# A two-block transformer layer on one core: memory and x loaded in both orientations, x's norm factor moved behind the products

## The chip, the core and the metric

The kernel runs on one core of a Trainium2 chip. The metric is the device time of one execution in microseconds (us). The engines in what follows are TensorE (PE in the profile; its weight loads are PEld), VectorE (DVE), ScalarE (ACT), GpSimd (POOL) and SyncE (SP), whose queue issues all loads and stores here.

## The reference, cut to what matters

Two transformer blocks on 256 tokens of width 1024, all in float32. Only the start of the first block is touched by the change:

```python
def rms_norm(x, g):
    xf = x * lax.rsqrt(jnp.mean(x * x, axis=-1, keepdims=True) + RMS_EPS)
    return xf * g

h = rms_norm(x, mix_norm_g)                    # x: 256 x 1024
proj = h @ w_in                                # 1024 x 4800
u_pool, q_down, kv_down, k_rope_in, xq, gate_logits = jnp.split(proj, ...)
y_pool = pool_mixer(u_pool, pool_w, pool_scale)
y_mla  = mla_branch(q_down, kv_down, k_rope_in, cos, sin, ...)
kv     = rms_norm(mem, mem_norm_g) @ w_mem_kv  # mem: 256 x 1024
y_mem  = memory_cross_attention(xq, kv)        # 4 heads of 128
gates  = sigmoid(gate_logits + gate_b)
x = x + (gates[0] * (y_pool @ w_br_pool) + gates[1] * (y_mla @ w_br_mla)
         + gates[2] * (y_mem @ w_br_mem)) @ w_out
x = x + hierarchical_moe(rms_norm(x, ffn_norm_g), ...)   # 32 experts, 2 per token
return second_block(x, ...)                    # attention and a gated FFN
```

## The kernel before, in words

**Arithmetic.** A float32 product is made of three passes over rounded halves: an operand a is split into a high part (rounded) and a low part (a minus the high part), and high x high, low x high and high x low are summed in PSUM. For weights, ACT makes the high half (`wh`, line 1309) and DVE the low half (`wl`, line 1720), a *piece* of up to 1024 columns at a time. There are four places for pieces (`PIECES`), so the split of piece n waits until TensorE has used piece n-4. In the program text `split_to(n)` splits all pieces up to n, and `stream(key)` walks over the pieces of one matrix and stays three pieces ahead (`AHEAD`).

**Orders.** Each engine has its own program and runs it strictly in order; semaphores named after the points they mark (`up`, `at`) tie them together. SP issues the weight loads in one list (`fetch(u)`), a unit being up to 1 MB. There are five raw places (`DENSE`), and from the sixth unit on `fetch` waits until DVE has made the last `wl` of the unit that held the place.

**The start.** `mem` comes as four column blocks of 256 KB into `H`, between the first four weight units. TensorE transposes each block (`turn_memory`, line 757), ACT and DVE make the halves `mT` from PSUM, scaled by the norm's gain G (lines 1358 and 1731), and `memory_keys` (line 777) multiplies the first half of `w_mem_kv` with them: four pieces, called 0 to 3 here. The token norm factor of `mem` is not in `mT`. It is applied where results leave PSUM: as a row for the keys (`spread` puts the factors on a diagonal on DVE, TensorE multiplies ones with it, and `spread_row` copies the row out), and as a scale for the values. Pieces 4 to 7 are the value half of `w_mem_kv`, pieces 8 to 11 are the columns `xq` of `w_in`, and after them come `qd`, `kvd` and the rest.

**x before.** x is loaded whole to `X`. ACT sums its squares (line 1318), POOL makes the factor (lines 2343 and 2346), DVE multiplies x by it into `H` (line 1824), TensorE transposes `H` in two groups of four tiles (line 645), and ACT and DVE make the halves `hT` from PSUM.

**The rotation's angles.** POOL makes the factors of mem and x first, in this order, and then computes the angles of the rotary embedding in some 24 small steps (lines 2361 to 2382). ACT takes their sine (line 1428). In ACT's program the sine stands after `whole(stream(("mkv", 1)))` and before `whole(stream("xq"))`, so the casts of the last xq piece and of the pieces after it stand behind the sine.

**Later stages.** The latents, the cross attention, the pooling and the gates of the first block, the experts (whose 100 MB are loaded while TensorE works), and the second block, which are not touched except for the places where x's factor now enters.

Of the kernel before, what the change touches and what calls it, by code (L numbers as in the profile page):

```python
# [26 lines left out]
MEM_AT = ((4, 0), (5, 0), (6, 0), (7, 0), (2, 0), (3, 0), (4, 1), (5, 1))  # L27
X_AT = ((4, 0), (5, 0), (6, 0), (7, 0), (4, 1), (5, 1), (6, 1), (7, 1))
# [170 lines left out]
def weights(a):  # L199
# [13 lines left out]
    wt.split(("mkv", 0), first[:, 0:2], first[:, 2:4], *(r[:, z:z + 2] for r in rest for z in (0, 2)))  # L213
# [65 lines left out]
def build(nc, wt, x, mem, positions, gate_b, w_gate_e, w_up_e, w_down_e, grow, w_route, b_route, rel_ext, cst, dense,  # L279
          out, force_general=False):  # L280
    with ExitStack() as ctx:
        program(nc, ctx, x, mem, positions, gate_b, grow, w_route, b_route, rel_ext, cst, out, wt, dense, w_gate_e, w_up_e,
                w_down_e, force_general)


def program(nc, ctx, x, mem, positions, gate_b, grow, w_route, b_route, rel_ext, cst, out, wt, dense,
# [27 lines left out]
    memory = H.rearrange("p i n -> p (i n)").rearrange("p (c m) -> p c m", c=4)  # L314
    memory_rows = memory.rearrange("p c (i n) -> p i c n", i=2)
# [44 lines left out]
    fr = [big[:, a:a + 64].rearrange("p (i c) -> p i c", i=2) for a in (8000, 8064, 8128)]  # L360
# [71 lines left out]
    def released(u):  # L432

        if wt.units[u][2]:
# [4 lines left out]
    s_load = {n: sem("s_" + n) for n in ("ident", "mem0", "mem1", "mem2", "mem3", "cst", "x", "pos", "gate0", "gate1",  # L439
                                         "gfin", "wr", "br", "pm", "pf", "bias", "out")}  # L440
# [12 lines left out]
    rr = rms("pre")[1][:, 2:4]  # L453
    krow = rt[:, 64:320]
# [28 lines left out]
    def sync(e, real):  # L483
# [34 lines left out]
        xs, ov = (v.rearrange("a (i p) n -> p (a i) n", p=P) for v in (x, out))  # L518
# [8 lines left out]
        load("cst", C[:, C_TRI:C_END], cst[:, C_TRI:C_END])  # L527
        load("pos", posi[:, :], positions)
        load("br", brow, b_route.to_broadcast([P, 36]))
# [35 lines left out]
        for u in range(DENSE, wt.dense_end):  # L565
# [42 lines left out]
    def tensor(e, real):  # L608
# [142 lines left out]
        def turn_memory(c):  # L751

            e.wait_ge(*have(f"mem{c}"))
            for k in (2 * c, 2 * c + 1):
                enter(MEM_AT[k][0], "lo", "mem", k)
                for i in range(2):
                    t = e.transpose(rows_at(MEM_AT[k])[:, P * i:P * i + P],
                                    memory_rows[:, i, c, P * (k % 2):P * (k % 2) + P], ident)
            t.then_inc(*up("turn", "mem", 2 * c))

        def memory_keys(c):


            q = wt.run["mkv", 0][c]
            h, l = halves(q)
            e.wait_ge(*at("wh", q))
            for n, (w, y) in enumerate(((h, mT[0]), (h, mT[1]), (l, mT[0]))):
                if n == 2:
                    e.wait_ge(*at("wl", q))
                for kk in range(2):  # L770
                    k = 2 * c + kk
                    if n < 2:
                        e.wait_ge(*at(("hi", "lo")[n], "mem", k))
                    for j in range(4):
                        if n == k == j % 2 == 0:
                            enter(j // 2, "kept xk", j // 2)
                        t = e.matmul(bank[j // 2][:, 256 * (j % 2):256 * (j % 2) + 256], w[:, kk, P * j:P * j + P], y[:, k],  # L777
                                     start=(n == k == j % 2 == 0), stop=(n == 2 and k == 7), skip_group_check=True)
                if n == 0 and c < 3:
                    turn_memory(c + 1)  # L780
# [5 lines left out]
        e.wait_ge(*have("ident"))  # L786
        turn_memory(0)
        warm(WARM[1], 0)
        for c in range(4):
            memory_keys(c)  # L790
        vals = tokens(("mkv", 1), 1, mT, ("kept", "xv"))
        next(vals)
        e.wait_ge(*have("cst"))
        spread("mem row", 4)
        next(vals)
# [1694 lines left out]
```

## Time and profile before

| | |
|---|---|
| median of 3 runs | 784.41 us (784.09 to 784.75) |
| span of the profiled execution | 782.0 us |
| its matmuls (PE) | 735.6 us busy |
| its DVE, ACT, POOL | 419.5, 335.4, 30.0 us busy |
| bytes moved | 203.97 MB |
| mean granted TensorE clock, as a share of full speed | 0.987 |

The span goes from the first to the last instruction, and the median of the times is 2.4 us above it; no separate time of the profiled execution is listed. Busy time says how long an engine worked, and not whether anything waited for it; this is read from the chain of waits and from the timelines. Times in the trace count from the start of the span.

### The profile page before, as it was taken

What the parts mean: (1) busy time and instruction counts of PE and PEld (TensorE: products, weight loads), DVE (VectorE), ACT (ScalarE), POOL (GpSimd) and SP (SyncE); (2) the same over time, 40 slices, a digit from 0 to 9 for tenths busy, and PEclk for the clock granted to TensorE, in tenths of its full rate; (3) what the DMA queues carried; (4) which work ended last, traced back from release to release, by engine and by line L of the source; (5) the groups of instructions that cost most, each with busy time, mean ns of one, the idle gap of its engine ahead of it and who ended that gap; (6) DMA issues with size and microseconds to landing.
All of it is one profiled execution on the core that took longest, in us unless ns stands there. A gap on an engine that the chain in (4) does not pass through costs nothing.

```text
span 782.0 us, 12563 instructions
## 1 busy us (share of the span) xinstructions
PE 735.6 (94%) x5192; PEld 608.0 (78%) x5192; DVE 419.5 (54%) x747; ACT 335.4 (43%) x603; POOL 30.0 (4%) x64
## 2 busy tenths in 40 slices
PE   8999999999999999998766889999999999999997
PEld 8898888888788876665543559999878888888885
DVE  4758746667667421110100207766658776777675
ACT  6766565454444421110110117566556534344433
POOL 0700000000000000000000001100001000000001
PEclk9999999999999999999988999999999999999999
DMA  8762567347968899999999998963424464555201
GB/s 309 287 256 95 196 248 267 124 175 266 360 229 335 345 395 422 420 421 419 421 421 421 421 416 326 408 222 137 162 109 148 146 244 162 176 201 178 92 1 54
DMA packets 32010, 203.97 MB, mean 261 GB/s; under 512 B 3792, under 2 KB 4176, under 8 KB 9936
## 3 DMA queue, kind: packets, MB, share of 16 engines
q1 hardware_dynamic: 31952, 203.15, 66.9%
q8 instruction: 42, 0.69, 0.4%
q14 instruction: 16, 0.13, 0.1%
HBM read 202.09 MB, written 1.05 MB: 260 GB/s over the span
## 4 chain that ended last, share of the span: by engine, by line
PE 86%; DMA 8%; ACT 3%; DVE 2%; issue 1%; SPq 1%; DVEq 0%; POOLq 0%; POOL 0%; ACTq 0%
PE ps L658 45%; PE ps L727 10%; DMA ext<-in_w_up_e 7%; PE ps L1022 6%; PE ps L730 5%; PE ps L999 3%; PE ps L1057 2%; PE ps L1047 2%; PE ps L777 2%; PE ps L1149 1%; PE ps L1163 1%; PE ps L1177 1%; PE ps L621 1%; ACT wh L1309 1%; ACT big L1560 1%
## 5 line engine op out<-in xcount | busy, mean ns | idle before, releaser
L1720 DVE TENSOR_TENSOR wl<-raw,wh 128x1024 fp32r<-128x1024 f32 (+3 forms) x180 | 213.2, 1200 | 129.6 <-ACT wh L1309 128.4
L1309 ACT CAST wh<-raw 128x1024 fp32r<-128x1024 f32 (+3 forms) x180 | 182.0, 1029 | 63.2 <-PE ps L658 44.0
L658 PE MATMUL ps<-wh,fra 128*128 128x512 f32 (+3 forms) x668 | 189.4, 369 | 0.4 <-DVE gb L1934 0.4
L658 PEld LDWEIGHTS ps<-wh,fra 128*128 128x128 f32 x668 | 118.7, 189 | 19.2 <-issue 1.0
L658 PE MATMUL ps<-wl,fra 128*128 128x512 f32 (+3 forms) x334 | 121.5, 364 | 0.0
L727 PE MATMUL ps<-fra,wh 128*128 128x512 f32 x352 | 110.7, 396 | 0.7 <-DVE fra L1731 0.7
L730 PEld LDWEIGHTS ps<-fra,wl 128*128 128x128 f32 x352 | 66.1, 188 | 15.5
L658 PE MATMUL ps<-wh,frb 128*128 128x512 f32 x240 | 74.4, 391 | 0.0
L658 PE MATMUL ps<-fra,wh 128*128 128x256 f32 x400 | 73.8, 286 | 0.1
L658 PEld LDWEIGHTS ps<-wl,fra 128*128 128x128 f32 x334 | 62.9, 188 | 9.6
L730 PE MATMUL ps<-fra,wl 128*128 128x256 f32 x352 | 69.3, 278 | 0.0
L658 PEld LDWEIGHTS ps<-fra,wh 128*128 128x128 f32 x400 | 62.3, 192 | 1.0 <-issue 0.6
L2129 DVE TENSOR_TENSOR S<-S,ps 128x256 f32<-128x256 f32 x8 | 3.4, 422 | 107.5 <-ACT S L1570 107.5
L658 PE MATMUL ps<-fra,wl 128*128 128x256 f32 x200 | 56.6, 283 | 0.0
L727 PEld LDWEIGHTS ps<-fra,wh 128*128 128x128 f32 x352 | 54.3, 189 | 1.6 <-issue 0.9
L1570 ACT ACTIVATE S<-ps 128x256 f32<-128x256 f32 x8 | 3.1, 383 | 114.6 <-PE ps L1022 114.6
L658 PEld LDWEIGHTS ps<-wh,frb 128*128 128x128 f32 x240 | 44.1, 188 | 8.5
L658 PE MATMUL ps<-wl,frb 128*128 128x512 f32 x120 | 46.8, 390 | 0.0
L1022 PE MATMUL ps<-ext,big 128*32 128x256 f32 x384 | 34.9, 427 | 7.5 <-DMA ext<-in_w_up_e 7.5
L1022 PE MATMUL ps<-big 128*32 128x256 f32 x192 | 32.7, 429 | 9.1 <-DMA ext<-in_w_up_e 9.1
L658 PEld LDWEIGHTS ps<-fra,wl 128*128 128x128 f32 x200 | 38.3, 192 | 0.0
L1022 PE MATMUL ps<-raw,big 128*32 128x256 f32 x448 | 29.6, 381 | 5.7 <-issue 2.0
(269 smaller groups left out, 938.7 us busy)
## 6 DMA issues: line engine op xcount, KB each, us to landing
raw<-in_dense SPq DMA_DIRECT2D x79, 1024.0 KB, 5.0
raw<-in_w_gate_e SPq DMA_DIRECT2D x25, 1024.0 KB, 26.0
ext<-in_w_up_e SPq DMA_DIRECT2D x24, 1024.0 KB, 26.1
ext<-in_w_down_e SPq DMA_DIRECT2D x16, 1024.0 KB, 23.5
raw<-in_dense SPq DMA_DIRECT2D x16, 512.0 KB, 7.1
big<-in_w_up_e SPq DMA_DIRECT2D x8, 1024.0 KB, 20.7
raw<-in_w_down_e SPq DMA_DIRECT2D x4, 1024.0 KB, 19.6
gb<-in_w_down_e SPq DMA_DIRECT2D x4, 1024.0 KB, 20.8
```

What stands on the lines that cost most here:

```text
L621: e.matmul(bank[b][:, 0:P], src[:, 0:P], src[:, 0:P], start=True, stop=True)
L658: t = e.matmul(o, a, w, start=first and n == 0, stop=final and n == 2, skip_group_check=not check)
L727: e.matmul(bank[b][:, :], h[:, kk, cols[j]], hT_both[:, k], start=(k == 0), stop=(k == 7), skip_group_check=True)
L730: t = e.matmul(bank[b][:, 0:256], l[:, kk, cols[j]], hT[0][:, k], start=False, stop=(k == 7), skip_group_check=True)
L777: t = e.matmul(bank[j // 2][:, 256 * (j % 2):256 * (j % 2) + 256], w[:, kk, P * j:P * j + P], y[:, k], start=(n == k == j % 2 == 0), stop= ...
L999: t = e.matmul(bank[2 + a][:, P * (kk % 4):P * (kk % 4) + P], H[:, i, P * kk:P * kk + P], hot[:, P * i:P * i + P], start=(i == 0), stop=(i ...
L1022: t = e.matmul(bank[0][32 * j:32 * j + 32, 256 * half_:256 * half_ + 256], XE[:, kk, 32 * j:32 * j + 32], slot_view(wt.raws[key, 4 * g + j ...
L1047: t = e.matmul(bank[2 + c][32 * j:32 * j + 32, :], AT[z][:, P * k + 32 * j:P * k + 32 * j + 32], slot_view(wt.raws["ed", 4 * g + j])[:, k, ...
L1057: t = e.matmul(turned(k), YE[k // 4][:, P * (k % 4):P * (k % 4) + P], CM, start=False, stop=False, skip_group_check=True)
L1149: t = e.matmul(causal_parts(bank[4 + z])[i], qT[o:o + 64, k, P * i:P * i + P], kT[o:o + 64, k, 0:P * (i + 1)], start=True, stop=True)
L1309: e.copy(halves(q)[0], piece_view(q)).then_inc(*up("wh", q))
L1720: e.tensor_tensor(l, piece_view(q), h.bitcast(F), ALU.subtract).then_inc(*up("wl", q))
```

## The change

1. `mem` and `x` are each loaded twice: once turned by the host (`mem_t` in five parts of 1, 1, 2, 2 and 2 tiles of 256 columns; `x_t` in one load of 1 MB), and once in rows as before (`mem` whole, to `H`). This adds 2 MB of loads.
2. The halves `mT` and `hT` are made from the turned tiles in SBUF. TensorE's 32 transposes at the start and one group of warming matmuls (6 in the program) go.
3. `hT` no longer holds x's norm factor. The factor is applied at each place where a product of x leaves PSUM: as a row for the queries (a second `spread` and `spread_row`), as a scale for q's and kv's latents and for the pool input, in the gates' addition, and in the cosine and sine of the keys, which POOL multiplies once.
4. The first four weight tiles are units of 256 KB of their own, so that the keys have six pieces, 0 to 5. The values are then pieces 6 to 9, xq 10 to 13, and qd starts with 14.
5. SP's list at the start is new: x and `x_t` come later in it.

```diff
-    wt.split(("mkv", 0), first[:, 0:2], first[:, 2:4], *(r[:, z:z + 2] for r in rest for z in (0, 2)))
+    wt.split(("mkv", 0), *(first[:, z:z + 1] for z in range(4)), *(r[:, z:z + 2] for r in rest for z in (0, 2)))
...
-        load("mem0", memory[:, 0], mem[0])
+        fetch(0)
         load("ident", C[:, 0:C_TRI], cst[:, 0:C_TRI])
-        for c in range(4):
-            fetch(c)
-            if c < 3:
-                load(f"mem{c + 1}", memory[:, c + 1], mem[c + 1])
+        memory_tiles(0)
+        fetch(1)
+        memory_tiles(1)
+        fetch(2)
+        memory_tiles(2)
+        fetch(3)
         fetch(4)
+        memory_tiles(3)
+        fetch(5)
+        memory_tiles(4)
+        fetch(6)
+        load("mem", H[:, :, :], ms)
+        load("cst", C[:, C_TRI:C_END], cst[:, C_TRI:C_END])
+        load("cst", posi[:, :], positions)
+        load("cst", brow, b_route.to_broadcast([P, 36]))
+        fetch(7)
+        load("xT", xT.rearrange("p k n -> p (k n)"), x_t)
+        fetch(8)
         load("x", X[:, :, :], xs)
...
-        turn_tiles("x", H, X_AT, range(4), [at("scaled", "x", i) for i in range(2)])
         whole(vals)
-        turn_tiles("x", H, X_AT, range(4, 8), [at("scaled", "x", i) for i in range(2)])
-        whole(features("xq", 0, hT, ("kept", "xq"), row=("lo", "x")))
+        queries = features("xq", 0, hT, ("kept x", "q"), row=("lo", "x"))
+        next(queries)
+        next(queries)
+        spread("x row", 5)
+        whole(queries)
...
+        e.wait_ge(*have("xT"))
+        high_rows("x", hT[0], xT, range(4), G_MIX)
+        split_to(values[3])
+        high_rows("x", hT[0], xT, range(4, 8), G_MIX)
+        split_to(values[3] + 1)
         e.wait_ge(*have("x"))
         for i in range(2):
             e.wait_ge(*(own() if i else at("squared", "mem", 1)))
             square(rms("x")[0][:, i:i + 1], X[:, i, :], junk, "x", i)
...
-        for j in range(2):
-            keep(xqT[:, 2 * j:2 * j + 2, :], two(j), at("piece", last["xq"]), "xq", j)
...
+        queries = stream("xq")
+        next(queries)
+        next(queries)
+        e.wait_ge(*at("factor", "x", 0))
+        spread("x row", x_factor)
+        spread_row("x row", 5)
+        whole(queries)
+        for j in range(2):
+            e.wait_ge(*at("piece", last["xq"]))
+            e.tensor_tensor(xqT[:, 2 * j:2 * j + 2, :], bank[j][:, :].rearrange("p (j n) -> p j n", j=2),
+                            krow.unsqueeze(1).to_broadcast([P, 2, 256]), ALU.mult).then_inc(*up("kept x", "q", j))
...
-                e.tensor_tensor(g, bank[2 + i][:, :], gbt[n % 2], ALU.add).then_inc(*up("biased", n, i))
+                e.scalar_tensor_tensor(g, bank[2 + i][:, :], x_factor[:, i:i + 1], gbt[n % 2], ALU.mult, ALU.add).then_inc(
+                    *up("biased", n, i))
...
+        e.wait_ge(*at("sines"))
+        for i in range(2):
+            t = e.tensor_scalar(cs_k[:, :, i, :], cs[:, :, i, :], x_factor[:, i:i + 1], None, ALU.mult)
+        t.then_inc(*up("pool step", "sines of keys"))
```

How the order moves on ACT, from the xq casts' side: first before, then after the change. A cast is the high half of a piece, the activation with table load is the sine.

```order
L1309 CAST wh<-raw 128x1024 [waits p_piece,s_slot2]
L1358 ACTIVATE fra<-ps,C 128x256 [waits p_turn] x4
L1425 ACTIVATE big<-ps,st 128x512 [waits p_piece,p_factor]
L1425 ACTIVATE big<-ps,st 128x512 [waits p_piece]
L1428 ACT_TABLE_LOAD
L1428 ACTIVATE cs<-cs 128x128 [waits p_angles]
L1309 CAST wh<-raw 128x1024 [waits p_piece]
L1309 CAST wh<-raw 128x768 [waits p_piece,s_slot3]
```

```order
L1360 ACTIVATE fra<-big,C 128x256 [waits s_xT]
L1360 ACTIVATE fra<-big,C 128x256 x3
L1312 CAST wh<-raw 128x1024 [waits p_piece]
L1360 ACTIVATE fra<-big,C 128x256 x4
L1312 CAST wh<-raw 128x1024 [waits p_piece,s_slot3]
L1321 ACTIVATE junk,st<-X 128x1024 [waits p_squared,s_x]
L1321 ACTIVATE junk,st<-X 128x1024 [waits p_squared]
L1312 CAST wh<-raw 128x1024 [waits p_piece]
L1312 CAST wh<-raw 128x1024 [waits p_piece,s_slot4]
L1433 ACTIVATE big<-ps,st 128x512 [waits p_piece,p_factor]
L1433 ACTIVATE big<-ps,st 128x512 [waits p_piece]
L1436 ACT_TABLE_LOAD
```

x's squares now stand after the halves of the turned x and after the cast of piece 10, two casts and the values' scaling ahead of the sine; behind the sine the order is as it was.

On DVE, the low halves of the xq pieces: first before, then after the change. The two TENSOR_SCALAR on `rt` are the diagonal of x's factors.

```order
L1731 SCALAR_TENSOR_TENSOR fra<-ps,C,fra 128x256 [waits p_hi] x4
L1720 TENSOR_TENSOR wl<-raw,wh 128x1024 [waits p_wh,s_cst]
L1720 TENSOR_TENSOR wl<-raw,wh 128x768 [waits p_wh] x4
L1785 TENSOR_REDUCE st<-ps 128x2 [waits p_scores]
L1787 TENSOR_SCALAR st<-st 128x2 [waits p_step]
```

```order
L1729 TENSOR_TENSOR wl<-raw,wh 128x1024 [waits p_wh] x3
L1729 TENSOR_TENSOR wl<-raw,wh 128x1024 [waits p_wh,s_cst]
L1729 TENSOR_TENSOR wl<-raw,wh 128x768 [waits p_wh]
L1752 TENSOR_SCALAR rt<-C,st 128x128 [waits p_factor]
L1752 TENSOR_SCALAR rt<-C,st 128x128
L1757 COPY rt<-ps 128x256 [waits p_spread]
L1729 TENSOR_TENSOR wl<-raw,wh 128x768 [waits p_wh,p_x_row]
L1729 TENSOR_TENSOR wl<-raw,wh 128x768 [waits p_wh]
L1850 TENSOR_TENSOR big<-ps,rt 128x512 [waits p_piece] x2
```

The diagonal now stands behind the low halves of piece 13 (1024 columns, the last of xq) and of piece 14 (768 columns, the first of qd).

On TensorE the new spread stands between the second and the third xq piece:

```order
L674 MATMUL ps<-fra,wh 128x256 x2
L674 MATMUL ps<-fra,wl 128x256
L669 MATMUL ps<-rt,C 128x128 [waits p_diag]
L669 MATMUL ps<-rt,C 128x128
L674 MATMUL ps<-fra,wh 128x256 [waits p_lo,p_wl]
```

Before, the four xq pieces ran without anything between them.

## Rows read from the trace of the kernel before

**Rows 1.** The page's first part: busy us (share of span) xinstructions.

```profile
PE 735.6 (94%) x5192; PEld 608.0 (78%) x5192; DVE 419.5 (54%) x747; ACT 335.4 (43%) x603; POOL 30.0 (4%) x64
```

**Rows 2.** Chain of waits, first 60 us: start us, us, what.

```profile
7.29 1.22 PE ps L777 x8
...
11.81 0.44 PE ps L757 x4
...
23.11 0.45 PE ps L653 x4
...
26.31 1.07 PE ps L645 x8
...
32.86 0.87 PE ps L645 x8
33.73 13.60 PE ps L658 x108
...
53.22 2.08 PE ps L658 x12
```

**Rows 3.** ACT's timeline: start us, us, engine line op out<-in xcount [idle before].

```profile
20.45 1.06 ACT L1318 ACTIVATE junk<-X 128x1024 f32<-128x1024 f32 x1
...
22.68 3.08 ACT L1309 CAST wh<-raw 128x1024 fp32r<-128x1024 f32 x3
...
33.77 1.57 ACT L1358 ACTIVATE fra<-ps,C 128x256 fp32r<-128x256 f32 x4 [2.49 <-PE ps L645]
...
38.87 0.31 ACT L1428 ACTIVATE cs<-cs 128x128 f32<-128x128 f32 x1 [1.07 <-POOL cs L2382]
39.09 2.50 ACT L1309 CAST wh<-raw 128x1024 fp32r<-128x1024 f32 x3
```

**Rows 4.** Five microseconds of loads, in the view by windows (last two: DMA share, GB/s).

```profile
20.00:25.00 5.00, 5.00 (x26) 4.22 (x26) 2.99 (x5) 4.92 (x8) 2.65 (x5) 1.00 1.02 431
```

**Rows 5.** POOL's timeline: x's factor done, then the angles.

```profile
23.79 0.18 POOL L2361 CAST st<-posi 128x2 f32<-128x2 int32 x1
24.08 2.65 POOL L2364 TENSOR_SCALAR big<-C,st 128x32 f32<-128x32 f32 x2
26.82 0.24 POOL L2369 TENSOR_SCALAR big<-big 128x64 f32<-128x64 f32 x1
...
29.31 1.04 POOL L2377 TENSOR_TENSOR cs<-big 128x64 f32<-128x64 f32 x1
...
34.78 0.24 POOL L2369 TENSOR_SCALAR big<-big 128x64 f32<-128x64 f32 x1
...
36.46 0.32 POOL L2377 TENSOR_TENSOR cs<-big 128x64 f32<-128x64 f32 x1
```

**Rows 6.** DVE's timeline.

```profile
21.71 0.47 DVE L1737 TENSOR_SCALAR rt<-C,st 128x128 f32<-128x128 f32 x2
...
31.66 2.47 DVE L1720 TENSOR_TENSOR wl<-raw,wh 128x1024 fp32r<-128x1024 f32 x2
...
40.22 4.07 DVE L1720 TENSOR_TENSOR wl<-raw,wh 128x1024 fp32r<-128x1024 f32 x4 [4.28 <-ACT wh L1309]
```

**Rows 7.** PE's timeline in the expert stage: the same 64 matmuls after two waits.

```profile
385.66 3.66 PE L1022 MATMUL ps<-raw,big 128*32 128x256 f32 x64 [1.94 <-DMA raw<-in_w_gate_e]
396.80 5.46 PE L1022 MATMUL ps<-ext,big 128*32 128x256 f32 x64 [7.48 <-DMA ext<-in_w_up_e]
```

**Rows 8.** Windows: stretch, PE PEld DVE ACT POOL busy, PEclk, DMA share, GB/s.

```profile
220.00:240.00 20.00, 20.00 (x94) 16.65 (x93) 13.25 (x16) 9.73 (x12) 0.00 (x0) 1.00 0.59 217
300.00:320.00 20.00, 18.54 (x217) 12.21 (x212) 2.69 (x7) 2.70 (x8) 0.00 (x0) 1.00 1.01 421
384.00:389.00 5.00, 3.34 (x64) 2.39 (x64) 0.00 (x0) 0.00 (x0) 0.00 (x0) 1.00 1.01 421
396.00:399.00 3.00, 2.20 (x24) 1.22 (x28) 0.00 (x0) 0.00 (x0) 0.00 (x0) 0.50 0.99 412
```

**Rows 9.** The waits of SP's own queue: us in total, times, longest us.

```profile
SPq L493 <- DVE wl L1720: 430.9, 83, 10.8
```

More of the change, by code:

```diff
@@ L564, in sync @@
             (("br", 1, 0), 1), (("br", 1, 1), 1), (("out", 0), 0), (("out", 1), 2)))}
-        for u in range(DENSE, wt.dense_end):
+        for u in range(9, wt.dense_end):
             if u in bias_at:
@@ L749, in attention, with memory_keys @@
                 yield
[L751 to L764, printed above, removed]
+        def memory_keys(q):
+            p = wt.pieces[q]
             h, l = halves(q)
@@ L769, in memory_keys @@
                     e.wait_ge(*at("wl", q))
-                for kk in range(2):
-                    k = 2 * c + kk
+                for kk in range(p.rows):
+                    k = p.k0 + kk
                     if n < 2:
@@ L1352, in high, with high_rows @@
                     t.then_inc(*up("hi", name, a, i))
+        def high_rows(name, dst, src, tiles, gcol):
+            for k in tiles:
+                e.activation(dst[:, k, :], src[:, k, :], ACT.Copy, scale=G[:, gcol + k:gcol + k + 1]).then_inc(
+                    *up("hi", name, k))
         def high_tiles(name, dst, table, tiles, group, gcol):
@@ L1396, in scalar @@
         e.copy(st[:, 95:96], gb[:, 0, 0:1])
-        e.wait_ge(*have("ident"))
-        for c in range(4):
-            if c:
-                split_to(c)
-            high_tiles("mem", mT[0], MEM_AT, (2 * c, 2 * c + 1), 2 * c, G_MEM)
-            if c == 0:
-                split_to(0)
-        split_to(4)
+        for c, (a, b) in enumerate(MEM_TILES):
+            split_to(b - 1 if b < 4 else 3 if b == 4 else b // 2 + 1)
+            if c == 0:
+                e.wait_ge(*have("ident"))
+            e.wait_ge(*have(f"memT{c}"))
+            high_rows("mem", mT[0], memT, range(a, b), G_MEM)
+        values = wt.run["mkv", 1]
+        split_to(values[0])
+        e.wait_ge(*have("mem"))
         for i in range(2):
@@ L1414, in scalar @@
             square(rms("x")[0][:, i:i + 1], X[:, i, :], junk, "x", i)
[L1415 to L1421 removed]
+        whole(stream(("mkv", 1)))
         e.wait_ge(*at("factor", "mem", 0))
@@ L1484, in pooling @@
             for i in range(2):
-                keep(uu[:, i, :], bank[2 + i][:, :], at("piece", last["pool"]) if i else at("piece", last["pool"], 0), "u", i)
+                e.wait_ge(*(at("piece", last["pool"]) if i else at("piece", last["pool"], 0)))
+                e.activation(uu[:, i, :], bank[2 + i][:, :], ACT.Copy, scale=x_factor[:, i:i + 1]).then_inc(
+                    *up("kept", "u", i))
             for g in range(5):
@@ L1805, in finish @@
             return take
-        for c in range(4):
-            if c:
-                split_to(c)
-            low_tiles("mem", mT, MEM_AT, (2 * c, 2 * c + 1), G_MEM)
-            if c == 0:
-                split_to(0)
-        split_to(5)
+        e.wait_ge(*have("ident"))
+        for a, b in MEM_TILES:
+            low_rows("mem", mT, memT, range(a, b), G_MEM)
+            split_to(b - 1 if b < 4 else 3 if b == 4 else b // 2 + 1)
+        values = wt.run["mkv", 1]
+        split_to(values[2])
         e.wait_ge(*at("factor", "mem", 0))
-        e.wait_ge(*have("ident"))
         spread("mem row", rms("mem")[1])
+        low_rows("x", hT, xT, range(4), G_MIX)
         spread_row("mem row", 4)
-        split_to(6)
-        e.wait_ge(*at("factor", "x", 0))
-        e.wait_ge(*at("turn", "mem", 6))
-        e.wait_ge(*at("squared", "mem", 1))
-        for i in range(2):
-            e.tensor_scalar(H[:, i, :], X[:, i, :], rms("x")[1][:, i:i + 1], None, ALU.mult).then_inc(*up("scaled", "x", i))
-        whole(stream(("mkv", 0)))
         for j in range(2):
@@ L2007, in routed @@
             return up("step", "route", n_route[0])
-        e.wait_ge(*have("br"))
         e.wait_ge(*at("factor", "h2", 0))
```

102 lines of the change are left out of this document (47 added, 55 removed).

## Prediction

> **What bounds the kernel now.** I read the page's busy times first: TensorE works in 94% of the span [rows 1]. Then the chain of waits for the first 60 us: from 7.29 us on every piece of it is a TensorE group [rows 2], so here a microsecond that TensorE is spared, or made to wait, is one of the span. Third, the timelines of ACT, POOL and DVE around 20 to 45 us [rows 3, 5, 6], to see which of their work comes just in time. The four xq pieces run from 33.73 us on. The group of 108 matmuls there is their 96 and 12 of qd, which alone take 2.08 us elsewhere, so the four take 11.52 us, 2.88 each, and xq ends at 45.25 [rows 2]. The sine runs at 38.87 after a wait of 1.07 for POOL's angles, the casts behind it start at 39.09, and DVE, which had stood still for 4.28 us, makes their low halves from 40.22 on [rows 3, 6]. The first of them, of the last xq piece, takes 1.2 us and is ready at 41.4, and TensorE wants it at 33.73 + 3 x 2.88 = 42.4. So the angles on POOL are only 1 us from binding. That is the place to follow.
>
> **What is removed.** TensorE loses three groups of transposes of 0.44 us inside the keys (a fourth lay before the chain's first matmul), and x's two groups, 1.07 and 0.87 [rows 2]: 3.3 us. The six warming matmuls go from a wait for the loads, at nothing. The first matmul comes earlier, since 480 KB have to be there for it and no longer 864: at most 2.4 us, if it comes at 4.9, when the warming ends and the first cast and tile can be done. The new spread costs 0.45, by the one of mem [rows 2]. On TensorE's own count that is -3.3 - 2.4 + 0.45 = -5.2 us. Nothing of it reaches the end if something later holds xq back.
>
> **What is moved: x comes late.** I count bytes. Before, 5462 KB stand ahead of the fifth whole unit (mem 1024, constants 342, weights 3072, x 1024). After, 5462 KB again stand ahead of the second unit of the values (both forms of mem 2048, constants 342, weights 3072). Before, that unit's first cast ran at 22.68 without waiting for a load [rows 3], so I put its landing at 22.6 in both. Behind it now come `x_t`, an xq unit and x, 1.05 MB each, at 431 GB/s [rows 4] 2.43 us apiece: `x_t` at 25.1, xq at 27.5, x at 29.9. ACT, from 25.1 on: four tiles 1.57, a cast 1.03, four tiles 1.57, a cast 1.03 (3.08 for three) [rows 3] = 30.3. It then finds x there. Its squares start at 30.3, where before they started at 20.45.
>
> **The chain from there.** From the squares' start to POOL's first step of the angles took 20.45 to 23.79 = 3.34 us [rows 3, 5]: 33.6. The angles took from there to the sine 15.08 us. I do not take this whole. Some POOL steps are three times as long as the same ones later (1.04 against 0.32 for line 2377), and this is when DVE makes low halves [rows 5, 6]. The second angle, with DVE idle, took from 34.78 to the sine at 38.87, 4.09 us. The first has one step more, 4.4. Ahead of both stand 3.03 us (23.79 to 26.82), in which two steps took 2.65 beside DVE [rows 5]; the low halves of pieces 11 and 12 fall there again, so I keep it. After them DVE has nothing to do until the sine. The angles then cost 3.03 + 4.4 + 4.09 = 11.5 us, and the sine starts at 45.1. The Trainium skill (SBUF — State Buffer, the practical consequences of its ports) says that a DVE instruction with two SBUF inputs contends with a GpSimd instruction that reads SBUF and that the second one blocks; by it DVE's idle time frees POOL and the 11.5 holds, while the whole old length of 15.08 would add 3.6 us. The trace's 1.04 against 0.32 agrees.
>
> Behind the sine, first the casts and low halves, as before: the first low half starts 1.35 us after the sine did (38.87 to 40.22). **The added wait** is the diagonal of x's factors: it is queued on DVE behind the low halves of piece 13 and of piece 14, which both stand behind the sine. Of 4.07 us for one of 1024 columns and three of 768 [rows 6], these two are 2.2. Then the diagonal, 0.47 [rows 6], and the spread, 0.45. On TensorE the spread is in front of the third xq piece, so not one but two pieces, 5.76 us, are held behind it, though piece 12's halves have long been ready. Sum: 45.1 + 1.35 + 2.2 + 0.47 + 0.45 + 5.76 = 55.4, against 45.25 before: **+10.1 us**.
>
> **TensorE's clock.** TensorE is done with the second xq piece between 38 and 39 (the squares end at 32.5, the cast of piece 11 at 33.6, its low half at 34.8, and the product 2.88 behind that or behind piece 10), and stands idle for some 10 us. In the expert stage the same 64 matmuls take 3.66 us after an idle time of 1.94, and 5.46 after one of 7.48, with a granted clock of 1.00 and 0.50 [rows 7, 8], that is 2.4 and 1.2 GHz. One such restart costs at least 1.8 us; I take 2.0, since here the work goes on without a pause. Total **+12.1 us**.
>
> **Parts at nothing.** The queries are copied out by DVE with a multiplication (two of 512 columns, as the keys are) where ACT copied. TensorE has a qd piece of 2.08 us in between, which hides either. The pool input, q's and kv's latents, their squares and the gates take one more scalar in the same instruction. The gates on DVE lie beside a TensorE that is fully busy [rows 8]; a price of at most 0.1 us per gate would give 0.6, and I take 0. POOL's two extra products follow the sine and are wanted at the keys' rotation, some 15 us later. The wait for the router's bias goes and was long fulfilled.
>
> **Does the delay reach the end?** The stage from 280 us on is bound by loads, share 1.01 at 421 GB/s, but at 220 to 240 the share is 0.59 [rows 8]. SP waits 430.9 us in 83 waits for a place that DVE's low halves free [rows 9], and these go at TensorE's pace. So loads do not run ahead in a stall: all of it moves by the same amount. 782.0 + 12.1 = 794.1 for the span, and with the 2.4 between it and the median, **796.5**.
>
> **The rivals.**
> - *The clock stays up*: +10.1, 794.5. Only the idle time of 7.48 with a clock of 0.50 speaks against it. The same number comes out if POOL's two steps of 2.65 are not held this time (-2).
> - *The angles are as slow as before*, 15.08, or x lands 3.6 us later, since the new loads have rows of 1 and 2 KB at first: +15.7, 800.1.
> - *The other side: nothing holds xq back.* TensorE keeps its own count, -5.2: 779.2. Place: the wait for the diagonal. It decides when the diagonal is ready before TensorE ends its second xq piece, near 38.5; the sine would have to run by 34, with x's squares begun at 19. With x behind 9.5 MB of loads I see no way. Were only the sine harmless, `x_t` at 25.1 would still set DVE's row: four tiles, the keys' row and copies, and the low half of piece 9 at about 30 and of piece 10 at 33; then 11.52 + 0.45 end at 45.1, no change: 784.3.
> - *The delay is made up later*, because loads get ahead after all and the load-bound stage takes less waiting: 784 to 790. Rows 9 speak against it.
>
> **How the numbers follow.** The forecast with the clock's fall 0.57, the clock up or POOL freer 0.15, the slow chain 0.14, made up later 0.07 (of it 0.02 within 0.2%), no change by `x_t` 0.03, faster 0.04. The range 790.5 to 800.5 takes in the first three and part of the fourth: 0.86 by these cases, and I leave the rest for what I have not seen. A measurement of this kernel can tell about 0.2%, 1.6 us, from no change. Faster 0.04, same 0.05, slower 0.91.
>
> **What would show it.** In the changed kernel: x's squares on ACT at about 30; POOL's cast of the positions at 33 to 34; the sine near 45; DVE's diagonal behind two low halves at 48 to 49; TensorE idle for about 10 us in front of the second spread, released by DVE, then matmuls at twice their length and a granted clock of 0.50; xq's end at 57 and from there the old timeline, some 12 us later. It is wrong if the sine runs before 38, if the spread waits less than 5 us, or if the expert stage starts with a smaller lag than xq ended with.

## The result and the profile after

| | before | after |
|---|---|---|
| median | 784.26 us (784.09 to 784.75, 4 runs) | 797.63 us (796.85 to 800.11, 4 runs) |
| ratio, 95% interval | | 1.0166 (1.0151 to 1.0182) |
| span of the profiled execution | 782.0 us | 795.1 us |
| mean granted TensorE clock | 0.987 | 0.979 |

The changed kernel is 1.7% slower. The forecast was 796.5, in a range of 790.5 to 800.5. The rest of this section follows the chain in the trace of the changed kernel from one end of the loss to the other.

The page's busy times of the changed kernel, to be held against [rows 1]: ACT, DVE and POOL do about what they did. TensorE is busy 3.0 us longer with 40 matmuls fewer, and the other 10 of the 13.1 us are waiting.

```profile
PE 738.6 (93%) x5152; PEld 610.1 (77%) x5152; DVE 421.1 (53%) x752; ACT 336.1 (42%) x603; POOL 27.5 (3%) x66
```

Whom TensorE waited for in the first 62 us of the changed kernel (us in total, times, longest):

```profile
PE ps L669 <- DVE rt L1752: 10.2, 1, 10.2
PE ps L783 <- ACT fra L1360: 2.0, 2, 1.3
PE ps L674 <- DVE wl L1729: 1.3, 1, 1.3
```

Its ACT timeline, which answers to [rows 3]: x's squares begin at 30.93 where they began at 20.45, and the sine, which had waited 1.07 us for POOL, now waits 8.35 behind its table load.

```profile
23.36 1.05 ACT L1312 CAST wh<-raw 128x1024 fp32r<-128x1024 f32 x1 [1.02 <-DMA raw<-in_dense]
25.84 1.71 ACT L1360 ACTIVATE fra<-big,C 128x256 fp32r<-128x256 f32 x4 [1.43 <-DMA big<-in_x_t]
...
30.93 1.06 ACT L1321 ACTIVATE junk<-X 128x1024 f32<-128x1024 f32 x1
...
45.97 0.31 ACT L1436 ACTIVATE cs<-cs 128x128 f32<-128x128 f32 x1 [8.35 <-POOL cs L2396]
46.19 2.49 ACT L1312 CAST wh<-raw 128x1024 fp32r<-128x1024 f32 x3
```

Its POOL timeline, for [rows 5]: the first step of the angles at 34.36; the two steps that had taken 2.65 take 1.59, and the cast of the positions is the slow one instead.

```profile
34.36 1.14 POOL L2375 CAST st<-posi 128x2 f32<-128x2 int32 x1
35.61 1.59 POOL L2378 TENSOR_SCALAR big<-C,st 128x32 f32<-128x32 f32 x2
...
39.00 0.32 POOL L2391 TENSOR_TENSOR cs<-big 128x64 f32<-128x64 f32 x1
...
45.70 0.24 POOL L2396 TENSOR_SCALAR cs<-cs 128x64 f32<-128x64 f32 x1
```

Its DVE timeline, for [rows 6]: idle for 10.72 us, the low halves of pieces 13 and 14, the diagonal, and at the end of xq the new product with the row (DVE waits 1.00 for it).

```profile
47.31 2.09 DVE L1729 TENSOR_TENSOR wl<-raw,wh 128x1024 fp32r<-128x1024 f32 x2 [10.72 <-ACT wh L1312]
49.33 0.48 DVE L1752 TENSOR_SCALAR rt<-C,st 128x128 f32<-128x128 f32 x2
...
58.39 1.29 DVE L1850 TENSOR_TENSOR big<-ps,rt 128x512 f32<-128x512 f32 x2 [1.00 <-PE ps L674]
```

TensorE in the changed kernel, and behind it the same engine's clock. The spread comes after 10.17 us of idle time. The second row is the first product of the cross attention (`x_scores`, a mark used from here on), which stood at 47.17 before:

```profile
49.86 1.23 PE L669 MATMUL ps<-rt,C 128*128 128x128 f32 x4 [10.17 <-DVE rt L1752]
...
60.28 1.02 PE L810 MATMUL ps<-big 128*128 128x256 f32 x4
```

```profile
44.00:54.40 10.40, 4.54 (x21) 4.54 (x22) 3.87 (x6) 2.71 (x4) 2.45 (x7) 0.51 0.36 112
```

That row is of the view by windows (busy time of PE, PEld, DVE, ACT, POOL, then granted clock, DMA share, GB/s): TensorE works only from 49.86 on there, at a clock of 0.51, the lower level of 1.2 GHz.

The lag then travels. I read the same instruction in both traces at three marks, and the end, before and after: the first `x_scores` 47.17 and 60.28 (+13.1), a gate's addition in DVE 207.26 and 220.56 (+13.3), the last mark of the expert stage (the last 32 products of a `w_down_e`) 468.70 and 480.96 (+12.3), and the end 782.0 and 795.1 (+13.1). Nothing is made up: the 1 us less at the expert mark is gone again at the end, and the stage in front of that mark differs by more than this from one execution to the next, as the table below shows.

### The profile page after: what moved, and what is told of

It is laid out like the page before. It is cut to its first block, busy times and chain, and to the rows that moved or that the text cites. A ratio compares the mean times of both kernels' runs of the same rounds, so it can differ in the third digit from the quotient of the medians.

```text
span 795.1 us, 12490 instructions
## 1 busy us (share of the span) xinstructions
PE 738.6 (93%) x5152; PEld 610.1 (77%) x5152; DVE 421.1 (53%) x752; ACT 336.1 (42%) x603; POOL 27.5 (3%) x66
## 4 chain that ended last, share of the span: by engine, by line
PE 76%; DMA 12%; ACT 4%; DVE 3%; POOL 2%; issue 2%; SPq 1%; DVEq 0%; POOLq 0%; ACTq 0%
PE ps L674 39%; PE ps L743 10%; PE ps L1025 5%; PE ps L746 5%; DMA raw<-in_w_gate_e 4%; DMA big<-in_w_gate_e 3%; DMA ext<-in_w_up_e 3%; PE ps L1002 2%; PE ps L1050 2%; PE ps L783 2%; DVE wl L1729 1%; SPq L493 1%; PE ps L1060 1%; DMA big<-in_rel_ext 1%; ACT wh L1312 1%
## 5 line engine op out<-in xcount | busy, mean ns | idle before, releaser
L1729 DVE TENSOR_TENSOR wl<-raw,wh 128x1024 fp32r<-128x1024 f32 (+4 forms) x182 | 213.5, 1188 | 137.3 <-ACT wh L1312 136.1
L1312 ACT CAST wh<-raw 128x1024 fp32r<-128x1024 f32 (+4 forms) x182 | 182.3, 1019 | 74.7 <-PE ps L674 51.1
L674 PE MATMUL ps<-fra,wh 128*128 128x256 f32 x400 | 75.4, 290 | 0.1
```

What stands on the lines that cost most here:

```text
L674: t = e.matmul(o, a, w, start=first and n == 0, stop=final and n == 2, skip_group_check=not check)
L1312: e.copy(halves(q)[0], piece_view(q)).then_inc(*up("wh", q))
L1729: e.tensor_tensor(l, piece_view(q), h.bitcast(F), ALU.subtract).then_inc(*up("wl", q))
```

## The experiments

The marks of all variants, in us of the profiled execution: the first product of the values (128x512, right behind the keys), the sine, the first and the third `x_scores`, the gate's addition, the last expert product; then the median with its number of runs and the ratio to the kernel before, which was timed anew beside each group of variants (784.94 beside the sine late, the diagonal first, the first warm gap and the angles first; 784.27 beside the nine early, the sine late in the kernel before, everything in the start and the warm start; 784.68 beside the rest).

| kernel | values | sine | 1st scores | 3rd scores | gate | last expert | median | ratio (95%) |
|---|---|---|---|---|---|---|---|---|
| before | 20.20 | 38.87 | 47.17 | 55.26 | 207.26 | 468.70 | 784.3 | |
| after | 20.56 | 45.97 | 60.28 | 68.37 | 220.56 | 480.96 | 797.63 (4) | 1.0166 (1.0151 to 1.0182) |
| after, again | 19.38 | 45.45 | 59.68 | 67.78 | 219.96 | 483.00 | 798.81 (5) | 1.0192 (1.0174 to 1.0211) |
| sine late | 20.87 | 48.93 | 48.64 | 57.21 | 209.39 | 470.77 | 786.75 (10) | 1.0027 (1.0007 to 1.0047) |
| diagonal first | 19.70 | 45.46 | 54.77 | 62.86 | 215.06 | 477.86 | 793.11 (4) | 1.0104 (1.0058 to 1.0150) |
| warm gap | 20.45 | 46.01 | 58.29 | 66.38 | 218.56 | 482.36 | 797.83 (4) | 1.0176 (1.0128 to 1.0224) |
| warm gap, again | 20.13 | 46.53 | 60.32 | 68.41 | 220.60 | 484.67 | 797.65 (5) | 1.0174 (1.0149 to 1.0199) |
| angles first | 19.51 | 37.68 | 49.95 | 58.04 | 210.23 | 472.19 | 788.03 (10) | 1.0033 (1.0013 to 1.0054) |
| sine late, nine early | 20.03 | 48.58 | 48.30 | 56.86 | 209.04 | 470.01 | 786.86 (12) | 1.0027 (1.0012 to 1.0043) |
| before, sine late | 20.02 | 44.43 | 46.99 | 55.09 | 207.11 | 473.44 | 785.14 (12) | 1.0005 (0.9990 to 1.0019) |
| everything in the start | 18.39 | 48.63 | 48.34 | 56.92 | 209.14 | 471.04 | 787.48 (12) | 1.0038 (1.0021 to 1.0055) |
| warm start | 19.25 | 48.12 | 47.82 | 56.41 | 208.62 | 470.80 | 786.96 (12) | 1.0033 (1.0014 to 1.0051) |
| all, split angles | 18.15 | 42.43 | 45.55 | 53.64 | 205.82 | 468.72 | 782.07 (8) | 0.9970 (0.9959 to 0.9981) |
| big first pieces | 20.30 | 48.14 | 47.85 | 56.42 | 208.61 | 468.79 | 784.89 (12) | 1.0005 (0.9994 to 1.0016) |

**Sine late.** The changed kernel, with ACT's sine moved behind the casts of the xq stream. Nothing else differs.

```diff
-        e.wait_ge(*at("angles"))
-        e.activation(cs[:, :, :, :], cs[:, :, :, :], ACT.Sin).then_inc(*up("sines"))
         whole(stream("xq"))
+        e.wait_ge(*at("angles"))
+        e.activation(cs[:, :, :, :], cs[:, :, :, :], ACT.Sin).then_inc(*up("sines"))
```

> The changed kernel with one move on ACT: the wait for the angles and the sine stand behind the casts of the xq pieces, no longer ahead of them. Theory (the delay is POOL's angles, handed on by the sine that stands in front of the casts of pieces 13 and 14): those casts run at about 36 to 38 us, the diagonal of x's factors is ready at 40, TensorE waits for it under 1 us where it waited 10.2, its clock stays up, xq ends at about 46.3 where it ended at 58.4. Time about 785.5, 12 us less than the changed kernel and within 2 us of the kernel before. Rival (x's late factor itself holds the spread, or the doubled loads do): x's factor is ready at 34.4 anyway, but if something behind it held the diagonal, the time would stay at 795 or more.

The wait at the second spread falls from 10.2 to 0.2 us, the clock does not fall, and 10.9 of the 13.4 us are gone. That the sine ahead of the last xq casts carries the loss is shown. In this kernel's PE timeline:

```profile
40.24 0.71 PE L669 MATMUL ps<-rt,C 128*128 128x128 f32 x4 [0.25 <-DVE rt L1752]
48.64 1.02 PE L810 MATMUL ps<-big 128*128 128x256 f32 x4
```

**Diagonal first.** The changed kernel, with the diagonal of x's factors on DVE ahead of the low halves of pieces 13 and 14.

```diff
+        e.wait_ge(*at("factor", "x", 0))
+        spread("x row", x_factor)
         queries = stream("xq")
         next(queries)
         next(queries)
-        e.wait_ge(*at("factor", "x", 0))
-        spread("x row", x_factor)
```

> The changed kernel with one move on DVE: the diagonal of x's factors stands ahead of the low halves of pieces 13 and 14. The sine stays where it is. Theory: TensorE gets its spread at about 39.6 us and can do piece 12 beside POOL's angles; only piece 13 waits, for its low half at 48.5. That takes away one piece (2.9), the second low half (0.9), the diagonal (0.5) and the spread (0.5 to 1.2 at the low clock) from the path; TensorE still stands idle for over 5 us and restarts at 1.2 GHz. xq ends at about 53.4 instead of 58.4; time about 792.6, 5 us less than the changed kernel. Rival (the diagonal's place does not matter, the sine alone does): no change from 797.6.

The spread and the third piece go through at once; the last xq piece then waits for its own low half behind the sine, 5.56 us, and the clock falls all the same. The scores come 5.5 us earlier than in the changed kernel, which is what the added wait's place costs. With the sine late they come another 6.1 us earlier (54.77 against 48.64), which is the sine's part, and 1.5 us stay (48.64 against 47.17 before). This kernel's PE timeline, where the first row of the last xq piece has 0.80 us for two products (0.40 is the length at full clock), then two windows:

```profile
48.01 0.80 PE L674 MATMUL ps<-fra,wh 128*128 128x256 f32 x2 [5.56 <-DVE wl L1729]
```

```profile
45.00:48.00 3.00, 0.00 (x0) 0.00 (x0) 1.27 (x2) 2.54 (x4) 1.20 (x4) 0.51 0.01 3
48.00:51.50 3.50, 3.49 (x16) 3.49 (x17) 2.99 (x4) 0.90 (x2) 0.00 (x0) 0.50 0.72 239
```

**Warm gap, twice.** The changed kernel with `warm(36, 5)`, 72 products of 128 columns whose result nobody uses, on TensorE ahead of `spread("x row", 5)`.

> The changed kernel with 36 small products of constants (128x128, some 0.25 us each, 9 us in all) put on TensorE ahead of the spread of x's factors, where it stands idle for 10.2 us. Their results are used by nothing. Theory: the wait for the diagonal is as long as before and ends at the same 49.9 us, but the granted clock does not fall, so that the spread and pieces 12 and 13 take 6.2 us and not 8.5: xq ends at about 56.1, time 2.3 us less, 795.3. Rival (the longer time behind the wait is no matter of the clock): no change, 797.6.

> The changed kernel with 36 warming matmuls ahead of the second spread once more: the clock stays up there, and the x-scores started 2.0 us earlier, but the first times showed nothing of it (797.8 against 797.6). Theory A (the 2 us reach the end, and four runs were too few to see it): 795.5, that is 2 us under the changed kernel of this call. Theory B (the expert stage, which the loads bind, takes them back): within 0.7 us of the changed kernel.

The changed kernel itself ran a second time beside the second one:

> The changed kernel once more, beside the next one on the same chip, for the question whether the clock's fall reaches the end: 797.5 (796.9 to 798.5), with the row of matmuls behind the second spread again at twice its length.

In the first profile the warming runs from 39.51 to 47.7, TensorE then waits 2.18 us, and the clock stays up: from the spread to the scores 8.39 us instead of 10.42. That prices the clock's fall at 2.03 us. In the second profile the same pause of 2.15 us ended with the lower clock, and it took 9.91 us, against 10.35 in the changed kernel's second profile. The windows from 50 to 54 us of the first and of the second (the clock is the third number from the end):

```profile
50.00:54.00 4.00, 4.00 (x34) 4.00 (x35) 1.38 (x2) 0.42 (x1) 0.00 (x0) 1.00 0.73 270
```

```profile
50.00:54.00 4.00, 3.59 (x18) 3.59 (x19) 1.74 (x4) 0.00 (x0) 0.00 (x0) 0.60 0.93 287
```

The times say little: 0.2 us above the changed kernel's first median, and 1.2 us below its second one, which ran beside it, with intervals that overlap. In the first profile the 2.0 us were still there at the gate (218.56 against 220.56) and were gone at the last expert product (482.36 against 480.96). Whether a kept clock is worth 2 us at the end isn't settled: a fixed number of warming products did not keep it in each execution. The Trainium skill (TensorE: Matmul & The Clock Gate, What's actually happening) says that the window in which the chip looks at TensorE's activity runs freely and that the moment of the rise to full clock at a kernel's start therefore varies from run to run. The page says it of the rise; here the fall varied as well, 1.00 and 0.60 after the same pause.

**Angles first.** The changed kernel, with POOL computing the angles ahead of x's factor (`root("x", ...)` behind them, and not before).

> The changed kernel with one move on POOL: the angles are computed ahead of x's factor, so they need not wait for x. Theory: they start at about 23.5 us beside a busy DVE and take 13 to 15 us as in the kernel before, the sine runs at 37 to 38.5, x's factor is ready a microsecond behind the angles, the diagonal at about 42, xq ends at 47.5 to 49. Time 787 to 788, some 10 us less than the changed kernel. If the angles take only 11.5 us here too (rival for the slow steps: they are not slowed by DVE), the sine runs at 35 and the time is 785.5. Rival (the doubled loads or DVE's added work make the time, not x's place ahead of the angles): 795 or more.

The sine runs at 37.68, in its old place on ACT, and costs nothing. x's factor is now late: TensorE waits 2.5 us in all for the diagonals. Two different repairs thus land within 1.3 us of each other, since each takes away the same wait.

**Before, sine late.** The control: the kernel before with the sine moved in the same way.

> The kernel before with the sine alone moved behind the xq casts on ACT. My reading is that before the change the angles came 1 us before they would bind, so that the sine's place costs nothing there: 784.3, within 0.2% of before. Rival (the late sine is a gain of its own, and would flatter the late-sine run of the changed kernel): 782 to 783. If the sine then comes late for its users, slower by up to 1 us.

By the ratio 0.4 us, inside the interval. So the late sine is no gain of its own that these runs can tell (the interval ends at 0.8 us below the kernel before), and the 1.0 us of slack that the prediction read at the start was slack.

**Three tries at the last 2.5 us.** What remains of the loss with the late sine? *Nine early* moves the cast and low half of piece 9 ahead of the turned x's tiles. *Warm start* has `warm(12, ...)` for `warm(7, ...)` ahead of the keys. *Everything in the start* has the warm start and besides

```diff
+        fetch(7)
         load("mem", H[:, :, :], ms)
...
-        fetch(7)
...
-        split_to(values[0])
+        split_to(values[3])
         e.wait_ge(*have("mem"))
```

on SP and ACT (the second unit of the values ahead of mem's rows), the same order on DVE, tiles 2 and 3 of mem between the casts of pieces 2 and 3, mem's row behind the third piece of the values, and piece 10 ahead of x's last four tiles.

> The changed kernel with the sine behind the xq casts on ACT, as in the run with the late sine, and with the cast and the low half of piece 9 ahead of the halves of the turned x on both engines. In the late-sine run TensorE still waited 1.2 us for the low half of piece 9. Theory (the rest of the loss is that wait): the wait goes and the time falls by about 1.2 us to 785.5, with the x-scores starting at about 47.5. Rival (turned x's tiles are then late instead, or the rest of the loss is elsewhere): no change against the late-sine run, 786.7.

> The late-sine run with twelve instead of seven warming matmuls at the start. In the changed kernel TensorE stood still from 4.3 to 5.6 us and its first 24 products of the keys then took 0.25 us each where later ones take 0.14 us, until 10.0 us. Theory: without that pause they take 0.14 us from 5.6 us on, but the next tile only lands at 10.2 us, so all of it goes into a longer wait there: no change, 786.7, keys ending at 20.7. Rival: the slower products do reach the end, and 1 to 2 us come back, 785.

> The changed kernel with everything in its start put where the loads allow: the sine behind the xq casts; twelve warming matmuls at the start in place of seven, so that TensorE works until its first product; tiles 2 and 3 of the turned memory made ready between pieces 2 and 3; the second unit of the values loaded ahead of mem's rows; pieces 8 and 9 ahead of mem's squares, mem's row behind the third piece of the values; piece 10 ahead of the last four tiles of x. Theory: TensorE's own count (5.2 us shorter than before) then shows in part, the keys ending at about 18.5 instead of 20.7 and xq at 43 to 45: x-scores at 45 to 47, time 782 to 784. Rival (2 MB more of loads at 430 GB/s take back whatever TensorE is spared): x-scores at 47 or later and 784 to 786.

All three kept the time of the late sine, 786.9 to 787.5, though the values began 0.8, 1.6 and 2.5 us earlier (two executions of the changed kernel differ by 1.2 us in this mark, 20.56 and 19.38, and their ends don't follow it). The gains went into small waits for x's low halves and factor (in *everything*, 2.3 and 1.3 us; its first scores, at 48.34, show the sign that its rival named, 47 or later, and its time is above the rival's 784 to 786). What stands behind these five runs (the late sine, these three, and *big first pieces* below) is where x's squares begin on ACT: 31.21, 30.89, 30.40, 30.93 and 30.44. The first scores come 17.41 to 17.43 us behind that in each, since the casts of pieces 11 to 14, their low halves, the diagonal and the spread in front of the third xq piece all follow x's squares. The sine comes 17.69 to 17.72 us behind it, and the third scores another 8.28 to 8.29. So nothing that is gained ahead of x's squares can reach either. The sine holds the third scores on its own as well: in the late-sine run TensorE waits 0.43 us in front of them, and they come 8.57 us behind the first scores instead of 8.09. The chain of waits of the late-sine run says why:

```profile
48.66 0.25 POOL cs L2396
48.93 0.31 ACT cs L1437
49.24 0.73 ACT wh L1312
49.99 0.96 DVE wl L1729
50.95 0.61 DVE st L1800
51.59 0.18 DVE st L1802
...
57.21 1.13 PE ps L810 x4
```

The sine had been moved out of the way of xq and stood in the way of the softmax. In these runs this costs only about 0.5 us, but had the first scores come earlier, the third would still have waited for it. It could not come before POOL's angles, and these took 14.3 us, not the 11.5 of the changed kernel: DVE, which there had stood still, now made low halves at the same time. Two groups that took 0.84 and 0.32 in the changed kernel take, in the late-sine run's POOL timeline:

```profile
37.90 2.18 POOL L2386 TENSOR_SCALAR big<-big 128x64 f32<-128x64 f32 x2
...
41.48 1.10 POOL L2391 TENSOR_TENSOR cs<-big,cs 128x64 f32<-128x64 f32 x1
```

**All, split angles.** So the last version adds to *everything* that POOL makes the first of the two angles between mem's factor and x's, and the second behind x's; ACT casts piece 11 ahead of x's squares; and the x row stands behind the third xq piece.

```diff
+            if f == 0:
+                e.wait_ge(*at("squared", "x", 1))
+                root("x", 0, 1024, 2)
...
+        split_to(values[3] + 2)
         e.wait_ge(*have("x"))
...
         next(queries)
         next(queries)
+        next(queries)
         spread("x row", 5)
```

> The run with everything in its start, and besides: POOL computes the first of the two angles ahead of x's factor and the second behind it; ACT casts piece 11 ahead of x's squares; the x factors' row stands behind the third xq piece. In the late-sine runs the chain of waits from 31 to 57 us was x's squares, POOL's angles, the sine at 48.1 to 48.9, a cast, a low half, the softmax of the first head and TensorE's third scores at 56.4 to 57.2, whatever had been gained ahead of it. Theory: this is what held four variants at 786.8 to 787.5; with the sine at about 42 the third scores start at 54 or before, x-scores at 45 to 46, and the time is 782.5 to 784. Rival (something behind, in the gates or the loads, makes up the 2.5 us): 786 or more with the same early rows.

782.07 us, 0.3% under the kernel before, the only version that beats both. Beside *big first pieces*, the late-sine kernel that was timed next to it, the first scores come 2.30 us earlier, the third scores 2.78, the gate 2.79, and the median is 2.82 lower. POOL's first angle fills a hole in which POOL had nothing to do, the second ends at 42.4, and the sine finds it done. Its POOL timeline has x's factor between them, its ACT timeline a sine without a wait, and TensorE begins the scores 1.6 us earlier than before:

```profile
24.93 0.18 POOL L2378 CAST st<-posi 128x2 f32<-128x2 int32 x1
...
31.52 0.24 POOL L2399 TENSOR_SCALAR cs<-cs 128x64 f32<-128x64 f32 x1
34.34 0.19 POOL L2364 TENSOR_SCALAR st<-st 128x2 f32<-128x2 f32 x1 [2.58 <-ACT junk L1323]
...
41.57 0.83 POOL L2399 TENSOR_SCALAR cs<-cs 128x64 f32<-128x64 f32 x1
```

```profile
42.43 0.31 ACT L1440 ACTIVATE cs<-cs 128x128 f32<-128x128 f32 x1
```

```profile
45.55 1.02 PE L812 MATMUL ps<-big 128*128 128x256 f32 x4
...
53.64 1.13 PE L812 MATMUL ps<-big 128*128 128x256 f32 x4
```

The split of the angles cannot have moved the first scores, for the sine stood behind the xq casts already. They move because piece 11's low half no longer keeps TensorE waiting (1.45 us in *everything*), and because the spread stands a piece later. Its diagonal is ready no earlier than in *everything* (DVE makes it at 39.45, against 39.42), but TensorE works through three xq pieces until then and doesn't wait, as its chain shows:

```profile
31.26 8.88 PE ps L674 x72
40.14 0.62 PE ps L669 x4
```

The split's part is that the third scores follow 8.09 us behind the first and no longer wait for the sine. The three changes ran only together, so this division is read from the trace and not shown by a run of each.

The profiled execution of this version, 784.19 us, is the longest of its eight, so its last marks are no measure of the gain.

**Big first pieces.** The late-sine run without part 4 of the change: the first weights in two units of two tiles.

```diff
-    wt.split(("mkv", 0), *(first[:, z:z + 1] for z in range(4)), *(r
+    wt.split(("mkv", 0), first[:, 0:2], first[:, 2:4], *(r
```

> The late-sine run with the first weights in two pieces of two tiles again instead of four of one tile, that is, the changed kernel without its small first pieces. Theory (what the first matmul gains is taken back by the wait for the next tile, since the loads bind until 20 us): the first product at about 6.5 us instead of 5.6, keys ending at 20.7 to 21.2, x-scores at 48.6 to 49, time 786.7 to 787.2. Rival (small pieces are what brings the start forward): keys and the end 1 us or more later, 788.

Both theories are wrong in the total: it is 1.9 us faster than the late-sine run in the median, with intervals of the ratios that overlap a little, taken in different comparisons. The values begin at 20.30 and with small pieces at 20.87, which is less than the scatter of this mark. So the small pieces bring nothing that can be seen. The marks up to the gate, though, are those of the warm start to 0.03 us (47.82, 56.41, 208.62), and that ran at 786.96. Whatever separates these two lies behind 208 us, where one of the two profiles is 2.0 us shorter by the last expert product; the variants differ there in how many units pass through the five raw places. That cause stays open.

## Why the prediction was right, step by step

**The sum.** Each step of the forecast stands in the trace; the start of each, predicted and measured:

| step | predicted | measured |
|---|---|---|
| cast behind the values' second unit | 22.6 | 23.36 |
| halves of the turned x | 25.1 | 25.84 |
| x's squares | 30.3 | 30.93 |
| POOL's first step of the angles | 33.6 | 34.36 |
| the sine | 45.1 | 45.97 |
| the angles, length | 11.5 | 11.6 |
| first low half behind the sine | +1.35 | +1.34 |
| two low halves | 2.2 | 2.09 |
| the second spread | 49.1 | 49.86 |
| xq's end, with the clock | 57.4 | 58.2 |
| lag of xq's end | +12.1 | +13.1 |
| end | 796.5 | 797.6 |

Most of the missing microsecond is the term of the loads: everything behind 22.6 comes 0.6 to 0.9 us late, and the spread 0.7. Another 0.2 is in the reading of the kernel before: 45.25 for xq's end came from the merged chain, while the first product behind xq starts at 45.08 there and at 58.19 after the change. As to the loads, the landing was taken from a cast that did not wait [rows 3], and the bytes ahead were counted as if they moved at the old rate. In the first ten microseconds the changed kernel moved 139 and then 341 GB/s (windows of 5 us) where the kernel before moved 173 and 375; that is 0.34 MB less, by estimate 0.8 us at 420 GB/s. SP also had to wait for a free place before it issued this unit, at 12.75. No run separates the two. The sizes of all waits and the order in which they came were as forecast.

**The angles.** The choice of 11.5 over 15.08 was right for the reason given, and the late-sine run shows the other side: with DVE working, 14.3. The slow steps were not those that I named, though. The two steps of 2.65 took 1.59 and the cast of the positions 1.14 instead of 0.18; that the sum came out is in part luck. The rule of the Trainium skill (SBUF — State Buffer, Who interferes with whom), by which a DVE instruction with two SBUF inputs contends with a GpSimd instruction that reads SBUF, agrees with these two traces: 0.32 against 1.10 for the same line, beside idle and working DVE. It is not always POOL that pays, though: in the last version its steps from 27.36 to 28.2 us took 0.37 and 0.32 as ever beside DVE's low halves of the turned x, and this group of DVE took 1.96 us instead of 1.68.

**The clock.** 2.0 was taken from two groups of the expert stage [rows 7]; it measured 2.03 at the scores. Whether it reaches the end stays open, as said above.

**The added wait.** One step was priced for its place and not for what it adds to the sine. *Diagonal first* removes 5.5 of the 13.1 us at the scores, which is the one more piece (2.88), the low half and diagonal in front, and a shorter stretch at the low clock. Of the remaining 7.6, the late sine removes 6.1.

**TensorE's own count.** The 5.2 us that TensorE was to be spared, the rival on the other side, did not even show at the keys' end. The first product came at 5.62 and not at 4.9, and the values began at 20.56 against 20.20. Its PE timeline shows where they went: products at twice their length, and then a wait.

```profile
5.62 2.04 PE L783 MATMUL ps<-fra,wh 128*128 128x256 f32 x8 [1.28 <-ACT fra L1360]
...
11.35 1.18 PE L783 MATMUL ps<-fra,wh 128*128 128x256 f32 x8 [0.67 <-ACT fra L1360]
```

The length of the products decides little here: in *angles first* and *diagonal first* the same eight took 1.26 and 1.25 us from 5.63 and 5.71 on, TensorE then waited 1.38 and 1.51 us where it waited 0.67, and the values began at 19.51 and 19.70; in the changed kernel's second profile, with the long products, they began at 19.38. The prediction asked whether these 5.2 us reach the end and never whether TensorE gets them. Even in the last version, with everything arranged for it, 1.6 of the 5.2 arrive at the scores.

**Parts at nothing.** A pair of gate additions takes 1.40 us instead of 1.28, that is 0.06 a gate, and from the scores to the gate mark it is 160.28 us against 160.09. The prices of nothing held.

**The delay reaches the end.** It did, by the marks above; SP still waited 444.0 us in 83 waits [rows 9]:

```profile
SPq L493 <- DVE wl L1729: 444.0, 83, 12.7
```

**"No change, by the turned x".** This rival was put at 784.3, if only the sine were harmless. The late-sine run is that case, and it came at 786.75, with the first scores 1.5 us and the third 2.0 us later than before. The rival had xq end at 45.1, and it ended at 46.5: DVE had the low half of piece 9 only at 31.1 and that of piece 10 at 33.9, where the rival had 30 and 33, xq ran from 34.07, and TensorE waited 0.25 us for the diagonal. It also left out the angles, slower beside a working DVE, and the softmax as their next user, which are the other 0.5 us.

## What to carry to other kernels

A step that is spared on the busiest engine is worth something only if what it stood in front of can come earlier as well; here a product's factor moved behind a late load, and an unrelated table function queued on the same in-order engine carried the delay to TensorE. When an instruction with a far-off producer stands in an engine's program, look at who is next in its queue, and after moving it, look who is next there. An otherwise idle engine's long chain of small steps can be cut in two, so that the urgent step goes between; here that was tried only together with two other moves.

## What the runs showed of the hardware that was not expected

- In the changed kernel the products from 5.62 to 10.0 us took 0.25 us each and later ones 0.14, though the column of the granted clock says 1.00 for these stretches. TensorE had paused for 1.28 us just ahead of them. With twelve warming matmuls in the program, a pause of 0.19 us, the first eight took 1.25 us and not 2.04. The pause alone does not decide it: behind pauses of 1.29 us (*angles first*) and 1.42 us (*diagonal first*) the same eight took 1.26 and 1.25, behind 1.47 us (*sine late*) 2.04. The factor is nearly that of the clock's two levels; that it is the clock is my reading, since the column doesn't show it.
- After the same pause of 2.15 to 2.18 us, in two executions of one kernel, the clock was 1.00 in one and 0.60 (over four microseconds) in the other.
- The stage of the experts, which the loads bind at 420 GB/s, takes a different time in each execution: from the gate's addition to the last expert product 260.2 to 266.3 us over the fourteen profiles here, and 260.4 and 263.0 in two of one kernel. A gain of 1 us ahead of it can't be read from one profile at its end.
- The table load and the sine took 1.28 and 0.31 us, and the switch back for the softmax another 1.28. Where the sine waited it was for POOL; the two switches cost less than the place in the queue (TensorE's 10.2 us).
